# A three-layer transformer stack on one core: return of x in quarters, pool sums on DVE, resting places of the modulation stream

## Chip, cores and metric

The kernel runs on one core of a Trainium2 chip. The metric is the device time of one execution in microseconds (us). The engines are named as in the profile: PE (TensorE), PEld (its weight loads), DVE (VectorE), ACT (ScalarE), POOL (GpSimd) and SP (SyncE, which here only issues DMAs).

## What is computed

A sequence of 512 tokens of width 2048 passes three layers, all in float32. Cut to what matters (layer 1 is attention, layer 2 pooling, layer 3 stick-breaking attention and retention; A, B are head groups):

```python
def modulation(c, w, b):                       # w: 2048 x 6144
    m = silu(c) @ w + b
    return m[:D], m[D:2*D], m[2*D:]            # shift, scale, gate

# layer 1
h = rmsnorm(x, pre_g) * (1 + scale) + shift
q, kv, z = split(h @ w_in)                     # 8 + 8 heads of 128, 2 + 2 kv heads
y = concat(dense_attention(qA, kA, vA), window_attention(qB, kB, vB, sink)) * silu(z)
x = x + gate * rmsnorm(y @ w_out, post_g)

# layer 2
u, z = split(h @ w_in)                         # 2048 + 2048
for g, w in enumerate((2, 4, 8, 16)):          # 4 groups of 512 columns
    mean = (sum of u over the tokens t - w//2 .. t + w//2 - 1, clipped) / count
    mixed_g = (mean - u_g) @ pool_w[g]
y = mixed * pool_scale * silu(z)
x = x + gate * rmsnorm(y @ w_out, post_g)

# layer 3
q, k, v, z = split(h @ w_in_2)                 # 8 stick-breaking, 8 retention heads
y = concat(stick_breaking(q, k, v), group_norm(retention(q, k, v))) * silu(z)
x = x + gate * (y @ w_out_2)
```

## The kernel before, in words

Activations lie transposed in SBUF: 16 tiles of 128 features by 512 tokens. To keep float32 accuracy every product is three products of rounded parts: an operand is split into a high part (HHI, WHI, PHI) and the rest (HLO, WLO, PLO), and hi x hi, lo x hi and hi x lo are added up in a PSUM bank G. Weights come in chunks of 128x4x256 (512 KB): SP loads a chunk into RAW, ACT casts it to WHI, DVE subtracts to WLO (stage "split"; three buffers each, so the split of chunk i+2 is asked for behind chunk i and waits until PE is done with chunk i-1), PE multiplies (stage "mm", 24 matmuls of 512 columns per chunk). A unit is 4 chunks and gives two G banks.

The order of all work is written out once by `make_plan` as one list of stages; each engine walks the list and executes its part of each stage, so the list is the order in every queue. Inside it run generators: those in `background` are stepped behind every quarter of a chunk (`step(background)`), the generator `mods` once behind every chunk (`unit`, L344). `finish` and `gated` run a generator to its end.

**Modulation.** `mod_stream` (L429) has 28 jobs of 8 steps. A step is a DMA of 512 KB into MWIDE (SP, asked for two steps ahead) and two DVE instructions that add a weighted row block to MACC (`mod_acc`); behind a job PE transposes MACC and DVE reduces it (`mod_sum`). `need_mods(t)` runs the stream on at once if job t isn't summed. `at["hold"]` stops the steps; before, it is set only in the first half of layer 3. Layer 1 has the units K and V (V token-major, `gemm_tok`, 72 matmuls of 256 columns per chunk), then 8 pairs of heads, each a q unit and a z unit with the attention of the pair in the background; the last z unit also has `first_splits`, which turns Y (the layer's gated result) into HHI and HLO for the output product.

**Output product.** `project_out` begins with `gemm_two`, which has the two first output units in the chunk order TWO, so that the last four tiles of Y are needed only from the seventh chunk. At that chunk `tail` finishes the background and puts four `x_back`: POOL issues four DMAs of 1 MB that bring the residual x from DRAM back to the quarters of XR, each with a semaphore `back[q]`. They wait until the scratch area under XR is free. In layers 1 and 2 the stage `o_more` (DVE) reads XR, in layer 3 the stage `o_copy` (DVE, `Y<-G,MOD,XR`), which also frees the G bank for PE; `write_out` sends the result out in four parts.

**Pool layer.** For group g: units u (2), the pool product of group g-1 (2 units of one chunk), units z (2). While the z units run, `pool_group(g)` is in the background: pairs on DVE (`pool_first`, UP 2172 columns), then g levels of doubling on POOL (`pool_level`), then on DVE the product with 1/count and the difference to u (`pool_mean`, both in one stage), then the splits PHI (ACT) and PLO (DVE).

Of the kernel before, what the change touches and what calls it, by code (L numbers as in the profile page):

```python
# [79 lines left out]
def build(nc, ctx, T, out):  # L80
# [137 lines left out]
    g_sum, g_ux, g_pad, g_pool = on_chip("g_sum", "g_ux", "g_pad", "g_pool")  # L218
# [93 lines left out]
    def make_plan():  # L312

        todo = []
        background = []
        gates = [[], []]
        at = {"load": 0, "split": 0, "use": 0, "unit": 0, "pair": 0, "heads": False, "hold": False}
# [32 lines left out]
        def unit(work, quiet=False):  # L350
            u = at["unit"]
            at["unit"] += 1
            n = len(units[u])
            at["pair"] += n // 8 + 1
            for c in range(n):
                i = at["use"]
                at["use"] += 1
                while at["split"] <= i:
                    split_next()
                work(u, i, c, c == n - 1)  # L360
                if not at["heads"]:
                    reduce_pending()
                while at["split"] < min(i + NS, len(chunks)):
                    split_next()
                if not (quiet and c >= n - 2 or at["hold"]):
                    step([mods])
            return u
# [35 lines left out]
        def gemm_two(layer, tail):  # L403
            first = at["pair"] % 2
            gated(first)

            def work(u, i, c, last):
                uu, k0 = TWO[c]
                pair = (first + uu) % 2
                if c == 3:  # L410
                    gated(pair)
                if c == 6:
                    tail()
                for nt in range(2):
                    for jj in range(2):
                        put("mm2", "y", layer, u, i, uu, k0, nt, jj, pair)
                        step(background)

            return unit(work), first
# [9 lines left out]
        def mod_stream():  # L429
            for _ in range(4):  # L430
                yield
            put("mod_load", 0)
            put("mod_load", 1)
            yield
            for t in range(len(mod_jobs)):
                for c in range(8):
                    reduce_pending()
                    put("mod_acc", t, c)
                    if 8 * t + c + 2 < 8 * len(mod_jobs):
                        put("mod_load", 8 * t + c + 2)  # L440
                    if c < 7:
                        yield
                pending.append(t)
                yield
            reduce_pending()
# [101 lines left out]
        pair = at["pair"] % 2  # L547
        u = gemm_tok(1, 6, pair)
        for i in range(3):
            put("v_copy", 1, i, pair, u)  # L550
# [76 lines left out]
        for p in range(8):  # L627
# [7 lines left out]
            if p == 7:  # L635
                h_unit = at["unit"]
                background.append(first_splits(1))
            u, pair = gemm("h", 1)
            silu(1, 2 * p, pair, u)

        def project_out(layer, h_unit):
            def tail():
# [5 lines left out]
                for q in range(4):  # L648
                    put("x_back", layer, q)

            u, first = gemm_two(layer, tail)
            for uu in range(2):
                for nt in range(2):
                    put("o_copy", layer, 2 * uu + nt, (first + uu) % 2, nt, u, (u, "two", uu, nt))
            more = products(layer, range(4), 3)
# [58 lines left out]
        def pool_group(g):  # L714
            put("pool_first", g)
            yield
            yield
            for level in range(g):
                put("pool_level", g, level)
                for _ in range(4):  # L720
                    yield
            put("pool_mean", g)
            for _ in range(5):
                yield
# [16 lines left out]
        for g in range(4):  # L741
# [5 lines left out]
            else:  # L747
                for uu in range(2):
                    u, pair = gemm("h", 2)
                    finish(task)  # L750
# [4 lines left out]
            background.append(task)  # L755
            for uu in range(2):
# [5 lines left out]
        finish(task)  # L762
        pool_product(3)
# [187 lines left out]
    def pool_program(e):  # L951
# [17 lines left out]
        for stage, *a in plan:  # L969
# [8 lines left out]
            elif stage == "x_back":  # L978
                layer, q = a
                scratch_free(layer)  # L980
                e.wait_ge(spill, layer)
                e.o.dma_start(XR[:, 4 * q:4 * q + 4, :], XS.ap()[:, 4 * q:4 * q + 4, :]).then_inc(
# [34 lines left out]
            elif stage == "pool_level":  # L1017
                g, level = a
                cur, nxt, lo, hi, sh = level_of(g, level)
                if level:  # L1020
                    e.wait_ge(g_pool, (g, level - 1))
                else:
                    e.wait_ge(v_pool, (g, "pairs"))
                add(UP[nxt][:, :, lo:hi], UP[cur][:, :, lo - sh:hi - sh], UP[cur][:, :, lo + sh:hi + sh]).then_inc(
                    *g_pool.up((g, level)))
# [352 lines left out]
    def dve_program(e):  # L1378
# [37 lines left out]
        for stage, *a in plan:  # L1416
# [307 lines left out]
            elif stage == "pool_first":  # L1724
                g, = a
                e.wait_ge(a_ev, ("u", g, 3))
                if g:
                    e.wait_ge(v_pool, (g - 1, "lo", 3))
                tt(UP[1][:, :, 1:544], UP[0][:, :, 0:543], UP[0][:, :, 1:544], ADD).then_inc(
                    *v_pool.up((g, "pairs")))  # L1730
            elif stage == "pool_mean":
                g, = a
                cur, dst = 3 - pooled_in(g), UP[pooled_in(g)][:, :, 16:528]
                if g:
                    e.wait_ge(g_pool, (g, g - 1))
                else:
                    e.wait_ge(v_pool, (g, "pairs"))
                e.wait_ge(rcd, g)
                for j in range(4):
                    tt(dst[:, j, :], UP[cur][:, j, 16:528], RC[:, :], MUL).then_inc(*v_pool.up((g, "rc")))  # L1740
                e.wait_ge(v_pool, (g, "rc"))
# [543 lines left out]
```

## Time and profile before

| | |
|---|---|
| time, median of 3 runs | 2621.2 us (2620.88 to 2621.57) |
| time of the profiled execution | 2625.44 us |
| its span | 2623.7 us |
| busy PE, PEld | 2551.8 us (97%), 2067.8 us (79%) |
| busy DVE, ACT, POOL | 1609.3 us (61%), 942.9 us (36%), 132.8 us (5%) |
| matmuls into G with 512 columns | 3 x 2624, mean 392 to 420 ns |
| chain that ended last, by engine | PE 87%, DVE 6%, DMA 3% |
| mean granted TensorE clock | 0.982 of full speed |

The span is what lies between the first and the last instruction; the time around it is 1.7 us more. A busy share is the time in which an engine had an instruction in work. Matmuls are pipelined: one of 512 columns lasts about 0.39 us and the next starts 0.23 us after it.

### The profile page before, as it was taken

How to read it: one execution, taken by the hardware profiler on the slowest of the kernel's cores; microseconds unless marked ns; L12 is line 12 of the kernel's file. 1: busy time of each engine (PE TensorE's matmuls, PEld its weight loads, DVE VectorE, ACT ScalarE, POOL GpSimd, SP SyncE). 2: the span in 40 equal slices, each digit the busy share in tenths (PEclk: the TensorE clock that was granted, in tenths of full speed). 3: DMA queues.
4: the chain of work that ended last, by engine and by line, in shares of the span. 5: the costliest groups of instructions: out<-in, count | busy, mean ns of one | idle time of the engine just before them, and what ended most of it. 6: DMA issues, size and time to landing. Idle time of an engine off the chain costs nothing.

```text
span 2623.7 us, 31292 instructions
## 1 busy us (share of the span) xinstructions
PE 2551.8 (97%) x12627; PEld 2067.8 (79%) x12627; DVE 1609.3 (61%) x2393; ACT 942.9 (36%) x1501; POOL 132.8 (5%) x121
## 2 busy tenths in 40 slices
PE   7999999999999999999999998999999999999998
PEld 4779777777777877888777887887888878878786
DVE  4445666677777768575787667446455567546432
ACT  4222444444444333332333333445354323223221
POOL 0000000000001103001021102000000000000000
PEclk8999999999999989999999998999999999999999
DMA  9934433444446644665647563222222255422432
GB/s 350 341 120 152 124 110 112 121 129 129 129 129 226 206 146 164 206 193 164 216 157 265 177 193 132 80 89 73 79 74 89 78 172 176 141 88 93 156 109 72
DMA packets 301074, 390.67 MB, mean 149 GB/s; under 512 B 11698, under 2 KB 237618, under 8 KB 297090
## 3 DMA queue, kind: packets, MB, share of 16 engines
q1 hardware_dynamic: 294800, 354.79, 43.3%
q0 software_dynamic: 6128, 33.89, 3.4%
q8 instruction: 100, 1.64, 0.3%
q14 instruction: 44, 0.36, 0.0%
q10 hardware_dynamic: 2, 0.00, 0.0%
HBM read 371.85 MB, written 16.78 MB: 148 GB/s over the span
## 4 chain that ended last, share of the span: by engine, by line
PE 87%; DVE 6%; DMA 3%; issue 1%; ACT 1%; SPq 1%; POOL 0%; DVEq 0%; ACTq 0%; POOLq 0%
PE G L1855 73%; PE S L1855 6%; PE OB L1855 5%; PE TB L1855 2%; PE TB L1858 2%; DVE MACC L1389 1%; DMA LATE<-in_ev_mod_w 1%; DMA MRAW<-in_ev_mod_w 1%; DVE WLO L1383 1%; DVE Y L1383 1%; DMA RAW<-in_w_out 1%; SPq L935 0%; DMA MWIDE<-in_w_ada 0%; PE OB L1858 0%; DMA MORE<-in_ev_mod_w 0%
## 5 line engine op out<-in xcount | busy, mean ns | idle before, releaser
L1855 PE MATMUL G<-HHI,WHI 128*128 128x512 f32 x2624 | 1102.5, 420 | 30.5 <-issue 7.8
L1855 PE MATMUL G<-HHI,WLO 128*128 128x512 f32 x2624 | 1032.2, 393 | 0.0
L1855 PE MATMUL G<-HLO,WHI 128*128 128x512 f32 x2624 | 1029.1, 392 | 0.0
L1383 DVE TENSOR_TENSOR WLO<-RAW,WHI 128x1024 fp32r<-128x1024 f32 x376 | 463.9, 1237 | 325.8 <-ACT WHI L1064 322.8
L1064 ACT ACTIVATE WHI<-RAW 128x1024 fp32r<-128x1024 f32 x376 | 395.7, 1054 | 605.4 <-PE G L1855 545.1
L1855 PEld LDWEIGHTS G<-HHI,WHI 128*128 128x128 f32 x2624 | 497.2, 189 | 147.2 <-issue 25.6
L1855 PEld LDWEIGHTS G<-HLO,WHI 128*128 128x128 f32 x2624 | 497.7, 190 | 110.6 <-issue 14.6
L1855 PEld LDWEIGHTS G<-HHI,WLO 128*128 128x128 f32 x2624 | 495.9, 189 | 109.0
L1389 DVE SCALAR_TENSOR_TENSOR MACC<-MWIDE,SC,MACC 128x512 f32<-128x512 f32 x420 | 339.6, 809 | 25.8 <-DMA MWIDE<-in_w_ada 11.1
L1855 PE MATMUL G<-WHI,HHI 128*128 128x256 f32 x640 | 185.3, 289 | 0.0
L1855 PE MATMUL G<-WLO,HHI 128*128 128x256 f32 x640 | 181.0, 283 | 0.0
L1855 PE MATMUL G<-WHI,HLO 128*128 128x256 f32 x640 | 181.0, 283 | 0.0
L1855 PEld LDWEIGHTS G<-WHI,HHI 128*128 128x128 f32 x640 | 122.5, 191 | 7.2 <-issue 6.3
L1855 PEld LDWEIGHTS G<-WHI,HLO 128*128 128x128 f32 x640 | 122.6, 192 | 1.9 <-issue 1.0
L1855 PEld LDWEIGHTS G<-WLO,HHI 128*128 128x128 f32 x640 | 122.6, 192 | 0.0
L1061 ACT ACTIVATE SQ<-SQ 128x512 f32<-128x512 f32 x144 | 90.8, 631 | 72.7 <-DVE SQ L1389 69.7
L1855 PE MATMUL S<-KTA,QR 128*128 128x256 f32 (+2 forms) x256 | 84.0, 451 | 2.6 <-ACT PB L1206 2.6
L1855 PE MATMUL OB<-PT,VV 128*128 128x512 f32 (+2 forms) x192 | 74.7, 539 | 0.0
L1206 ACT ACTIVATE PB<-S,SM 128x512 f32<-128x512 f32 (+1 forms) x32 | 23.7, 741 | 136.1 <-DVE SM L1386 136.1
L1386 DVE TENSOR_SCALAR TM<-TB 128x512 f32<-128x512 f32 (+1 forms) x28 | 18.8, 672 | 85.7 <-ACT TY L1061 85.7
L1855 PEld LDWEIGHTS S<-KTA,QR 128*128 128x128 f32 x256 | 47.9, 191 | 29.5 <-issue 15.3
L1206 ACT ACTIVATE PB<-S,SM,COL 128x768 f32<-128x768 f32 x32 | 31.7, 992 | 109.0 <-DVE SM L1386 109.0
(268 smaller groups left out, 2335.0 us busy)
## 6 DMA issues: line engine op xcount, KB each, us to landing
RAW<-in_w_in SPq DMA_DIRECT2D x128, 512.0 KB, 3.8
MWIDE<-in_od_mod_w SPq DMA_DIRECT2D x96, 512.0 KB, 4.7
MWIDE<-in_w_ada SPq DMA_DIRECT2D x96, 512.0 KB, 4.8
RAW<-in_ev_w_in SPq DMA_DIRECT2D x80, 512.0 KB, 3.6
RAW<-in_od_w_in SPq DMA_DIRECT2D x64, 512.0 KB, 3.8
MWIDE<-in_ev_mod_w SPq DMA_DIRECT2D x32, 512.0 KB, 4.6
RAW<-in_ev_w_out SPq DMA_DIRECT2D x32, 512.0 KB, 4.3
RAW<-in_od_w_out SPq DMA_DIRECT2D x32, 512.0 KB, 4.1
```

Of the source, the lines that this page charges most:

```text
L1061: return e.o.activation(o, i, fn, bias=bias, scale=scale)
L1064: return e.o.activation(o, i, ACT.Copy, scale=scale)
L1206: e.o.activation(PB[n % 2][:, lo:768], S[:, lo:768], ACT.Exp, bias=nm, scale=1.0 if banded(h) else q_root_of(h, qt), accum_out=SM[:, i + 1 ...
L1383: return e.o.tensor_tensor(o, a, b, op)
L1386: return e.o.tensor_scalar(o, a, s1, s2, op0, op1) if op1 else e.o.tensor_scalar(o, a, s1, None, op0)
L1389: return e.o.scalar_tensor_tensor(out=o, in0=a, scalar=s, in1=b, op0=op0, op1=op1)
L1855: return e.o.matmul(o, l, r, start=start, stop=stop, skip_group_check=True)
L1858: return e.o.transpose(o, i, IDN[:, :])
```

## The change

Three parts. (1) `tail` asks only for the first quarter of x; a generator asks for the other three, each 8 background steps (two chunks) apart, and every `x_back` also waits on PE until the chunk before the current one is done. (2) `pool_level` moves from POOL to DVE, `pool_mean` is cut into `pool_mean` and `pool_diff`, and the stages of `pool_group` stand 4 background steps apart (3 in group 3). (3) `mod_stream` starts without its four empty steps; it makes a second step behind each chunk of the V unit and behind the second chunk of each u unit of groups 1 to 3; it rests from the last z unit of the heads to the fourth chunk of `gemm_two`, and during the z units of group 3.

```diff
@@ -215,7 +215,7 @@
         "v_silu")
     v_ysp, v_ux, v_tile, v_pool, v_res, v_st, v_out, v_xy = on_chip(
         "v_ysp", "v_ux", "v_tile", "v_pool", "v_res", "v_st", "v_out", "v_xy")
-    g_sum, g_ux, g_pad, g_pool = on_chip("g_sum", "g_ux", "g_pad", "g_pool")
+    g_sum, g_ux, g_pad = on_chip("g_sum", "g_ux", "g_pad")
 
     XS = nc.dram_tensor("x_spill", [P, KT, SEQ], F32)
     MUL, ADD, SUB, MAX, MIN = ALU.mult, ALU.add, ALU.subtract, ALU.max, ALU.min
@@ -314,7 +314,7 @@
         todo = []
         background = []
         gates = [[], []]
-        at = {"load": 0, "split": 0, "use": 0, "unit": 0, "pair": 0, "heads": False, "hold": False}
+        at = {"load": 0, "split": 0, "use": 0, "unit": 0, "pair": 0, "heads": False, "hold": False, "extra": ()}
         scored = []
         summed = set()
         pending = []
@@ -364,6 +364,8 @@
                     split_next()
                 if not (quiet and c >= n - 2 or at["hold"]):
                     step([mods])
+                    if c in at["extra"]:
+                        step([mods])
             return u
 
         def gemm(kind, layer, quiet=False):
@@ -409,6 +411,8 @@
                 pair = (first + uu) % 2
                 if c == 3:
                     gated(pair)
+                if c == 4:
+                    at["hold"] = False
                 if c == 6:
                     tail()
                 for nt in range(2):
@@ -427,8 +431,6 @@
             return unit(work)
 
         def mod_stream():
-            for _ in range(4):
-                yield
             put("mod_load", 0)
             put("mod_load", 1)
             yield
@@ -545,7 +547,9 @@
         task = chain([norm_rope(("k", 2), False), norm_rope(("k", 3), False)])
         background.append(task)
         pair = at["pair"] % 2
+        at["extra"] = (0, 1, 2, 3)
         u = gemm_tok(1, 6, pair)
+        at["extra"] = ()
         for i in range(3):
             put("v_copy", 1, i, pair, u)
         finish(task)
@@ -635,6 +639,7 @@
             if p == 7:
                 h_unit = at["unit"]
                 background.append(first_splits(1))
+                at["hold"] = True
             u, pair = gemm("h", 1)
             silu(1, 2 * p, pair, u)
 
@@ -645,13 +650,19 @@
                 if layer == 2:
                     for k in range(12, KT):
                         put("y_split", layer, k, h_unit)
-                for q in range(4):
-                    put("x_back", layer, q)
+                put("x_back", layer, 0, at["use"] - 2)
+
+            def rest_back():
+                for q in range(1, 4):
+                    for _ in range(8):
+                        yield
+                    put("x_back", layer, q, at["use"] - 2)
 
             u, first = gemm_two(layer, tail)
             for uu in range(2):
                 for nt in range(2):
                     put("o_copy", layer, 2 * uu + nt, (first + uu) % 2, nt, u, (u, "two", uu, nt))
+            background.append(rest_back())
             more = products(layer, range(4), 3)
             for uu in range(2, 8):
                 if layer == 3:
@@ -712,16 +723,20 @@
         put("pads")
 
         def pool_group(g):
+            apart = 3 if g == 3 else 4
             put("pool_first", g)
+            for _ in range(apart):
+                yield
+            for level in range(g):
+                put("pool_level", g, level)
+                for _ in range(apart):
+                    yield
+            put("pool_mean", g)
+            for _ in range(apart):
+                yield
+            put("pool_diff", g)
             yield
             yield
-            for level in range(g):
-                put("pool_level", g, level)
-                for _ in range(4):
-                    yield
-            put("pool_mean", g)
-            for _ in range(5):
-                yield
             for j in range(4):
                 put("pool_split", g, j)
                 if j % 2:
@@ -746,13 +761,16 @@
                         put("u_copy", 0, 2 * uu + nt, (first + uu) % 2, nt, (u, "two", uu, nt))
             else:
                 for uu in range(2):
+                    at["extra"] = (1,)
                     u, pair = gemm("h", 2)
+                    at["extra"] = ()
                     finish(task)
                     for nt in range(2):
                         put("u_copy", g, 2 * uu + nt, pair, nt, (u, nt))
                 pool_product(g - 1)
             task = pool_group(g)
             background.append(task)
+            at["hold"] = g == 3
             for uu in range(2):
                 if g == 3 and uu == 1:
                     h_unit = at["unit"]
@@ -760,6 +778,7 @@
                 u, pair = gemm("h", 2)
                 silu(2, 4 * g + 2 * uu, pair, u)
         finish(task)
+        at["hold"] = False
         pool_product(3)
 
         need_mods(4 + 11)
@@ -976,9 +995,10 @@
                 e.o.dma_start(XS.ap()[:, 4 * q:4 * q + 4, :], XR[:, 4 * q:4 * q + 4, :]).then_inc(
                     *spill.up((1, q), *([1] if q == 3 else []), by=16))
             elif stage == "x_back":
-                layer, q = a
+                layer, q, i = a
                 scratch_free(layer)
                 e.wait_ge(spill, layer)
+                e.wait_ge(p_gemm, i)
                 e.o.dma_start(XR[:, 4 * q:4 * q + 4, :], XS.ap()[:, 4 * q:4 * q + 4, :]).then_inc(
                     *back[q].up(layer, by=16))
             elif stage == "o_copy":
@@ -1014,15 +1034,6 @@
                 if g:
                     e.wait_ge(v_pool, (g - 1, "rc"))
                 e.o.dma_start(RC[:, :], T["t_rcnt"][g]).then_inc(*rcd.up(g, by=16))
-            elif stage == "pool_level":
-                g, level = a
-                cur, nxt, lo, hi, sh = level_of(g, level)
-                if level:
-                    e.wait_ge(g_pool, (g, level - 1))
-                else:
-                    e.wait_ge(v_pool, (g, "pairs"))
-                add(UP[nxt][:, :, lo:hi], UP[cur][:, :, lo - sh:hi - sh], UP[cur][:, :, lo + sh:hi + sh]).then_inc(
-                    *g_pool.up((g, level)))
             elif stage == "tables3":
                 e.wait_ge(*x_done(2, 0))
                 e.o.dma_start(CS[:, :], T["t_rope_b"][0]).then_inc(*rope.up("cs3", by=16))
@@ -1728,16 +1739,22 @@
                     e.wait_ge(v_pool, (g - 1, "lo", 3))
                 tt(UP[1][:, :, 1:544], UP[0][:, :, 0:543], UP[0][:, :, 1:544], ADD).then_inc(
                     *v_pool.up((g, "pairs")))
+            elif stage == "pool_level":
+                g, level = a
+                cur, nxt, lo, hi, sh = level_of(g, level)
+                e.wait_ge(v_pool, (g, "level", level - 1) if level else (g, "pairs"))
+                tt(UP[nxt][:, :, lo:hi], UP[cur][:, :, lo - sh:hi - sh], UP[cur][:, :, lo + sh:hi + sh], ADD).then_inc(
+                    *v_pool.up((g, "level", level)))
             elif stage == "pool_mean":
                 g, = a
                 cur, dst = 3 - pooled_in(g), UP[pooled_in(g)][:, :, 16:528]
-                if g:
-                    e.wait_ge(g_pool, (g, g - 1))
-                else:
-                    e.wait_ge(v_pool, (g, "pairs"))
+                e.wait_ge(v_pool, (g, "level", g - 1) if g else (g, "pairs"))
                 e.wait_ge(rcd, g)
                 for j in range(4):
                     tt(dst[:, j, :], UP[cur][:, j, 16:528], RC[:, :], MUL).then_inc(*v_pool.up((g, "rc")))
+            elif stage == "pool_diff":
+                g, = a
+                dst = UP[pooled_in(g)][:, :, 16:528]
                 e.wait_ge(v_pool, (g, "rc"))
                 tt(dst, dst, UP[0][:, :, 16:528], SUB).then_inc(*v_pool.up((g, "mean")))
             elif stage == "pool_split":
```

## Rows read from the trace of the kernel before

**Rows 1.** Waits of TensorE: releaser, us in total, times, longest us

```profile
PE G L1855 <- DVE Y L1389: 8.1, 3, 6.1
```

**Rows 2.** Timeline of TensorE: start us, us, instruction, [idle before <-releaser]

```profile
775.42 0.59 PE L1855 MATMUL S<-KTA,QR 128*128 128x384 f32 x1 [2.56 <-ACT PB L1206]
793.48 0.50 PE L1855 MATMUL G<-HHI,WHI 128*128 128x512 f32 x1 [3.98 <-DVE HLO L1383]
1248.25 0.50 PE L1855 MATMUL G<-HHI,WHI 128*128 128x512 f32 x1 [1.16 <-DVE WLO L1383]
1255.57 0.50 PE L1855 MATMUL G<-HHI,WHI 128*128 128x512 f32 x1 [1.59 <-DVE WLO L1383]
1351.61 0.50 PE L1855 MATMUL G<-HHI,WHI 128*128 128x512 f32 x1 [2.17 <-DVE WLO L1383]
1368.94 0.33 PE L1858 MATMUL TB<-IDN,MACC 128*128 128x128 f32 x1 [0.67 <-DVE MACC L1389]
1391.07 0.50 PE L1855 MATMUL G<-PHI,WHI 128*128 128x512 f32 x1 [1.83 <-DVE Y L1389]
2472.64 0.76 PE L1855 MATMUL G<-HHI,WHI 128*128 128x512 f32 x1 [6.10 <-DVE Y L1389]
```

**Rows 3.** Windows: busy us per engine, then PEclk, DMA share, GB/s

```profile
794.00:799.00 5.00, 5.00 (x17) 3.89 (x17) 2.48 (x5) 0.28 (x1) 0.00 (x0) 0.66 0.54 168
1391.00:1396.00 5.00, 4.93 (x15) 3.90 (x16) 5.00 (x9) 2.49 (x5) 0.02 (x1) 0.66 0.24 88
2472.60:2477.60 5.00, 4.96 (x14) 4.01 (x15) 1.87 (x3) 0.60 (x1) 0.28 (x1) 0.51 0.35 105
2458.00:2462.00 4.00, 4.00 (x19) 3.34 (x18) 1.40 (x2) 0.00 (x0) 0.00 (x0) 1.00 1.02 421
1232.00:1276.00 44.00, 41.25 (x181) 33.53 (x180) 40.29 (x40) 14.95 (x21) 9.36 (x3) 1.00 0.57 175
```

**Rows 4.** Timeline of DVE at the end of the heads

```profile
770.55 1.53 DVE L1389 SCALAR_TENSOR_TENSOR MACC<-MWIDE,SC,MACC 128x512 f32<-128x512 f32 x2
779.33 1.53 DVE L1389 SCALAR_TENSOR_TENSOR MACC<-MWIDE,SC,MACC 128x512 f32<-128x512 f32 x2
792.74 0.69 DVE L1383 TENSOR_TENSOR HLO<-Y,HHI 128x512 fp32r<-128x512 f32 x1
```

**Rows 5.** Window of one chunk of the token-major V unit

```profile
206.20:214.80 8.60, 8.60 (x74) 8.60 (x73) 3.25 (x4) 1.06 (x1) 0.00 (x0) 1.00 0.77 247
```

**Rows 6.** Timelines of POOL and DVE, pool groups 2 and 3

```profile
1237.62 8.88 POOL L953 TENSOR_TENSOR UP<-UP 128x2164 f32<-128x2164 f32 x2 [93.93 <-DVE UP L1383]
1238.58 8.47 DVE L1389 SCALAR_TENSOR_TENSOR MACC<-MWIDE,SC,MACC 128x512 f32<-128x512 f32 x2
1337.41 8.48 DVE L1389 SCALAR_TENSOR_TENSOR MACC<-MWIDE,SC,MACC 128x512 f32<-128x512 f32 x2
1345.81 5.75 DVE L1383 TENSOR_TENSOR WLO<-RAW,WHI 128x1024 fp32r<-128x1024 f32 x1
```

**Rows 7.** Groups of DVE by line: busy us, mean ns, idle before

```profile
L1383 DVE TENSOR_TENSOR WLO<-RAW,WHI 128x1024 fp32r<-128x1024 f32 x376 | 463.9, 1237 | 325.8 <-ACT WHI L1064 322.8
L1383 DVE TENSOR_TENSOR UP<-UP,RC 128x512 f32<-128x512 f32 x16 | 10.0, 686 | 0.0
L1383 DVE TENSOR_TENSOR UP<-UP 128x2172 f32<-128x2172 f32 x4 | 9.7, 2414 | 3.7 <-ACT UP L1064 3.7
L1383 DVE TENSOR_TENSOR UP<-UP,UP 128x2048 f32<-128x2048 f32 x4 | 9.2, 2292 | 0.1
```

**Rows 8.** Chain that ended last, eight chunks of 24 matmuls: start, us

```profile
1278.08 43.56 PE G L1855 x192
```

**Rows 9.** Timelines of POOL and ACT in the last output product

```profile
2454.11 2.10 POOL L982 DMA_DIRECT2D XR<-x_spill  x4 [33.28 <-issue]
2469.52 1.06 ACT L1064 ACTIVATE WHI<-RAW 128x1024 fp32r<-128x1024 f32 x1 [13.01 <-DMA RAW<-in_w_out]
```

**Rows 10.** View of tile XR, 2440 to 2480, four returns of x

```profile
DMA to landing us min/median/max: 5.2/9.2/13.5
```

## The prediction

> **What bounds the kernel now.** I read the profile in this order: the table of engine busy time, the waits of TensorE, the timeline of TensorE around each of them, then the timelines of DVE, ACT and POOL just before. TensorE (PE) is busy 97% of the span and almost every piece of the chain that ends last is a matmul into a G bank, so a step is worth something only if it removes time in which PE stands still, or a stretch at the lower clock behind it. DVE is busy 61%: its mean says nothing, its place in each PE wait does.
>
> In the stages that the diff touches, PE has eight waits over 0.5 us [rows 1, 2]; the others lie in the intro, at the two layer boundaries and in the retention heads. Two lie at the end of the heads (2.56 and 3.98 us), two in pool group 2 (1.16, 1.59), three in and behind pool group 3 (2.17, 0.67, 1.83), and one in the last output product (6.10, the largest of the three waits of [rows 1]). Together 20.1 us. Behind three of them the granted clock is lower for a while: in 5 us it is 0.66 behind 793.5, 0.66 behind 1391, 0.51 behind 2472.6 [rows 3]. A share of 0.66 is part of the 5 us at 1.2 and the rest at 2.4 GHz. That costs 5 x 0.34 = 1.7, 1.7, and 5 x 0.49 = 2.45 us, 5.85 in all. The most the change could give is thus 25.9 us.
>
> **Modulation rests at the end of the heads.** One step of the modulation is two DVE instructions on MACC, 1.53 us together and 1.45 from its start to the start of what follows [rows 4]. Before: one step behind each chunk. After: none behind the four chunks of the last z unit and the first four of the output product; they are made up by starting four chunks earlier and by a second step in each of four chunks of the token-major V unit. Counting the generator through: before, 106 chunk steps up to the end of the layer-1 output less 5 that only load make 101 accumulations; after, 106 + 4 - 8 less 1, again 101. Twelve jobs need 96, so need_mods pulls nothing forward, and in the heads the count is exactly 8 higher, the same phase of a job. In the V unit PE waits for nothing in the trace and DVE is busy 3.25 of the 8.6 us that a chunk takes [rows 5], so the steps added there (two per chunk, 2.9 us) are hidden; if that cover were short, a late WLO would cost PE at most one step, 1.5 us.
>
> At 772.9 PE waits for scores whose exp waits for DVE. With the step at 770.55 gone DVE can run the split at once, but the silu piece behind it still waits for ACT: I trace it to about 772.0 instead of 772.69, so 0.7 is gained of 1.45. At 789.5 PE waits for the last of the y splits before its third chunk, DVE 792.74 [rows 4]. From 776 to 793 DVE works nearly without pause, so the removed step at 779.33 moves it by its whole 1.45, on top of the 0.7. Sum 2.2 us. The waits that stay (about 4.3 us) are softmax round trips between DVE and ACT. The lower clock behind them may stay too, I count half: 0.85. Bounds: 0 and 6.5 + 1.7.
>
> **Running sums on DVE.** POOL takes 4.4 us for one level, and meanwhile DVE's modulation step, 1.53 us elsewhere, lasts 8.47 and 8.48 us, and one split 5.75 instead of 1.24 [rows 6, 7]. So the level costs DVE nearly POOL's whole time though it runs on POOL: 8.47 - 1.53 = 6.9 us in group 2, and 6.95 + 4.5 = 11.5 us in group 3. A level on DVE isn't in the trace; the same form with 8 columns more is, 2.41 us [rows 7]. Six levels at 2.4 (1, 2, 3 in groups 1 to 3) put 4.8 us on DVE in group 2 and 7.2 in group 3 in place of 6.9 and 11.5. Bounds of a level: 2.3 (the subtraction of 2048 columns, [rows 7]) and 4.4, POOL's.
>
> The Trainium skill, SBUF — State Buffer, section "SBUF: two separate sides", says that DVE and GpSimd share one port pair by an exclusive lock, whoever starts first holding it for its whole instruction. By that rule the cost in group 2 is POOL's full 8.9 us less what was already running, against 6.9 from the row; the trace agrees. By the same rule a level on DVE would hold POOL in turn, and POOL has nothing there but one small table load.
>
> The larger part is order. In group 2 the split of the fourth chunk is queued behind POOL's two levels, and the next behind mean and difference at once: hence 1.16 and 1.59. After, the stages stand 4 steps, one chunk, apart. Eight chunks of 24 matmuls take 43.56 us, one 5.45 [rows 8]; DVE's work in it is split 1.24 + step 1.45 + level 2.41, or mean 4 x 0.63 (0.69 each, overlapping a little) in its place: 5.2 at most. A split is two chunks ahead and can start when the chunk before is done: with 1.06 for ACT's WHI and its own 1.24 about 8 us of room. The first chunk of the second z unit holds difference, four splits of the pool, one silu and a split and step: 8.5 us, which that room covers with about 0.5 us to spare. Over the stretch DVE is already 40.3 of 44 us busy [rows 3], 6.9 of it blocked, so I keep 0.5 us of new wait. Group 2 gives 2.75.
>
> In group 3 the spacing is 3 and the modulation rests for the eight chunks, 8 x 1.45 = 11.6 us of DVE less on top of 11.5 - 7.2 = 4.3. The tightest point is now the first chunk, with pairs, one level and its split due 10.9 us in; they end about 10.5 us in (today DVE starts the pairs 4.6 us into group 2, behind the same kind of job sum that group 3 gets now: + 2.33 + 2.33 + 1.2). DVE then stays ahead, the silu before the last pool product starts some 4 us earlier, and the waits 2.17, 0.67 and 1.83 go: 4.67 us, with the 1.7 us of lower clock. The two extra steps per group 1 to 3 stand in u chunks where DVE has only a split and then two steps, 1.24 + 2.9 of 5.45 us; their loads were issued a chunk before. The count is 163 instead of 165 behind group 3, and 193 instead of 195 where 192 are needed: nothing is forced. Pools together: 2.75 + 4.67 + 1.7 - 0.5 = 8.6. Bounds: 0 and 9.1.
>
> **Return of x in quarters.** Four DMAs of 1 MB already exist; all are issued at 2454.1 to 2455.7. The weight load issued beside them lands 14 us later, so WHI waits 13.01 us for it [rows 9], and DVE's split and then its first Y follow in order: PE stands from 2466.54. With the engines of the DMA at 421 GB/s [rows 3], 4 MB + 0.5 MB need 11 us; 1 MB + 0.5 MB need 3.7. The first quarter landed in 5.2 even in the crowd [rows 10]. After: the first quarter waits until the sixth chunk is done (about 2455.4, 1.3 later) and lands by 2462; the load lands by 2461; WHI may start when its buffer is free, chunk 7 done, 2461.1; WLO to 2463.5, Y to 2464.2; PE needs it at 2466.5. The wait of 6.10 goes with 2.3 us to spare, and the clock stays up: 2.45. Sum 8.55. Bounds 0 and 8.55 (the first quarter as late as 13.5 us gives nothing). What is behind the new wait in POOL's queue: the copies of x_out and, in layers 1 and 2, the adds of squares. Quarter 1 is issued when the second chunk of the next unit is done and needed (o_more 4, or o_copy 4 in layer 3) 11 us later at the earliest; at 5 to 9 us per quarter that holds by 2. In layers 1 and 2 no PE wait follows the burst now, so nothing is gained there.
>
> **Sum.** 2.2 + 0.85 + 8.6 + 8.55 = 20.2 us. The profiled execution took 2625.44 us (span 2623.7), so 2605.2 for it; it stands 4.2 above the median 2621.2, which gives 2601.
>
> **Rivals.**
> (1) The end of layer 3 is held by DVE's order or by the first quarter itself, not by the load: PE still waits 3 to 6 us and the clock falls. For it: Y also needs back[0]. Against: 5.2 us of landing. Gives 2.5 instead of 8.55: 2607. Chance 0.10.
> (2) The pools stay bound by DVE: the busy share of 0.92 and the 0.5 us margins speak for it, the removed blocking against it. Pools give 1: 2609. Chance 0.10.
> (3) Slower. In the first two chunks of the second z unit of groups 1 to 3, ACT and DVE pass silu and pool splits to and fro, with a level's worth of work more queued on DVE; if each of these six chunks is 4.5 us late, PE stands 27 us and the clock falls three times, 5 us: 32 in place of the pools' 9.1, against 2.2 + 0.85 + 8.55 = 11.6 gained elsewhere, so 11.3 slower, 2632.5. It decides from 3.5 us per chunk (21 + 5 - 9.1 - 11.6 = 5.3). Against it: group 1 has no wait today although its POOL level blocks DVE. Chance 0.05.
> (4) The change does nothing measurable: waits move to the next dependency everywhere. Chance 0.05: 2619.
>
> **How the numbers follow.** Forecast 0.70. What the measurement tells from no change is about 0.2%, 5.2 us. Faster: forecast, (1), (2): 0.90; same 0.05; slower 0.05. Range: all waits and clocks gone, 2595.3, would be the bottom; the top takes in (1) and (2) with some of both, 2612. Range 2595 to 2612.
>
> **What would show it.** Right: no PE row with a wait from 2440 to 2500 and a granted clock of 1.00 there; WHI's wait for w_out gone; MACC pairs at 1.5 us and DVE UP rows of 2.4 us one chunk apart; no WLO wait from 1230 to 1395; the wait of 3.98 down to about 2.6. Wrong: a PE wait on WLO in a second z unit, a Y of the last product waiting for XR, o_more waiting for XR in layers 1 or 2, or waits of PE for WLO in the first 100 us behind the intro.

## The result, and the profile after

The changed kernel takes 2612.57 us (median of 7 runs, 2606.37 to 2614.91), the kernel before beside it 2621.05 (7 runs). The ratio is 0.9965, 95% interval 0.9956 to 0.9975: 9 us faster, where 20.2 were forecast, and 0.57 us above the range.

The profiled execution took 2612.22 us (span 2610.1), close to its median. That of before lay 4.2 us above its own, so the two profiles differ by 13.2 us (13.6 in span). I aligned the two traces by their matmuls into G (10,032 in each) and read how far the one is ahead at each place. Less than 0 is a gain, in us (rounded; the lines add up to 13.4):

```
stretch                          profiles   forecast   PE waits that went or came
up to the last heads                -1.1        0
end of the heads                    -4.9      -3.05    2.56 went; 3.98 became 2.92
first layer boundary                +1.4        0      none came
pool groups 2 and 3                -10.8      -8.6     1.16, 1.59, 2.17, 0.67, 1.83 went
layer-2 output product              +6.2        0      3.99 CAME
second boundary, score heads        +0.1        0
retention heads                     +4.3        0      0.88, 0.36, 1.07, 0.88 CAME
layer-3 output product              -8.6      -8.55    6.10 went
```

So what was meant to go went, and two new groups of waits came. Waits of TensorE after (releaser, us in total, times, longest us). The row of [rows 1] for Y is gone. A row for HLO has two waits in it, of which the longer is new, and rows for MACC and WLO stand for the retention heads:

```profile
PE G L1872 <- DVE HLO L1394: 6.9, 2, 4.0
PE TB L1875 <- DVE MACC L1400: 1.8, 2, 0.9
PE G L1872 <- DVE WLO L1394: 1.4, 2, 1.1
```

Timeline of TensorE after, the rows that answer to [rows 2] and the new ones:

```profile
787.63 0.79 PE L1872 MATMUL G<-HHI,WHI 128*128 128x512 f32 x1 [2.92 <-DVE HLO L1394]
1417.31 0.77 PE L1872 MATMUL G<-HHI,WHI 128*128 128x512 f32 x1 [3.99 <-DVE HLO L1394]
2128.99 0.66 PE L1875 MATMUL TB<-IDN,MACC 128*128 128x128 f32 x4 [0.88 <-DVE MACC L1400]
2191.64 0.50 PE L1872 MATMUL G<-HHI,WHI 128*128 128x512 f32 x1 [0.36 <-DVE WLO L1394]
2198.45 0.50 PE L1872 MATMUL G<-HHI,WHI 128*128 128x512 f32 x1 [1.07 <-DVE WLO L1394]
2232.51 0.65 PE L1875 MATMUL TB<-IDN,MACC 128*128 128x128 f32 x4 [0.88 <-DVE MACC L1400]
```

Windows after (busy us per engine, PEclk, DMA share, GB/s). The places of [rows 3] in pool group 3, the last output product and group 2: 1.00 in all three, and DVE 37.0 us busy over group 2 (40.3 before). The third row is the new wait: half of 5 us idle, the rest near 1.2 GHz. Behind the wait that stays at the heads (787.63) the granted clock is 0.72 over 5 us, 0.66 before.

```profile
1384.00:1389.00 5.00, 5.00 (x24) 4.14 (x23) 3.63 (x6) 1.06 (x1) 0.00 (x0) 1.00 0.78 263
2460.00:2465.00 5.00, 5.00 (x28) 4.13 (x27) 1.31 (x2) 0.60 (x1) 0.55 (x1) 1.00 0.30 95
1415.00:1420.00 5.00, 2.69 (x6) 2.15 (x7) 4.96 (x8) 0.00 (x0) 0.00 (x0) 0.55 0.89 321
1226.00:1270.00 44.00, 44.00 (x197) 36.40 (x196) 37.02 (x41) 16.98 (x23) 0.54 (x1) 1.00 0.56 168
```

What DVE does ahead of the new wait (timelines of DVE and POOL after):

```profile
1413.35 0.69 DVE L1521 TENSOR_REDUCE MOD<-TB 128x4 f32<-128x512 f32 x1 [7.49 <-PE TB L1875]
1413.45 0.53 POOL L1002 DMA_DIRECT2D XR<-x_spill  x1 [168.65 <-PE G L1872]
1414.16 1.22 DVE L1394 TENSOR_TENSOR WLO<-RAW,WHI 128x1024 fp32r<-128x1024 f32 x1
1415.30 0.48 DVE L1397 TENSOR_SCALAR MACC<-MWIDE,SC 128x512 f32<-128x512 f32 x1
1415.81 0.75 DVE L1400 SCALAR_TENSOR_TENSOR MACC<-MWIDE,SC,MACC 128x512 f32<-128x512 f32 x1
1416.48 2.49 DVE L1394 TENSOR_TENSOR HLO<-Y,HHI 128x512 fp32r<-128x512 f32 x4
```

Every eighth modulation step ends a job. PE then transposes MACC (L1875) and DVE sums the result (`mod_sum`, L1521). DVE works two chunks ahead of PE, so it stands for 7.49 us until PE has come to these transposes. Behind the sum in DVE's queue are a split, the next job's first step and only then the four splits HLO 12 to 15. PE wants these directly behind its transposes: it waits from 1413.32 to 1417.31. Before, the sum lay two chunks earlier in the order (timeline of DVE before):

```profile
1417.93 0.69 DVE L1510 TENSOR_REDUCE MOD<-TB 128x4 f32<-128x512 f32 x1 [2.28 <-PE TB L1858]
1428.13 2.49 DVE L1383 TENSOR_TENSOR HLO<-Y,HHI 128x512 fp32r<-128x512 f32 x4
```

In the retention heads it is another neighbour, read off the two traces alone. The job's last step (MACC, 2127.41) is queued behind a chain of DVE work that begins at 2122.03, and PE, which is to transpose this MACC, waits 0.88 us for it:

```profile
2122.03 0.69 DVE L1397 TENSOR_SCALAR TM<-TB 128x512 f32<-128x512 f32 x1 [0.97 <-ACT TY L1072]
2127.41 1.53 DVE L1400 SCALAR_TENSOR_TENSOR MACC<-MWIDE,SC,MACC 128x512 f32<-128x512 f32 x2
```

Counted in the order of work (c=0 is the first chunk), the layer-2 output product has these DVE stages behind its third to sixth chunk, and the last line just ahead of its seventh, which reads HLO 12 to 15:

```
        before (165 steps ahead)      after (163 steps ahead)
c=2     last step of job 20           step
c=3     SUM, step                     step
c=4     step                          last step of job 20
c=5     step                          SUM, step
c=6     splits 12-15, x_back          splits 12-15, x_back
```

### The profile page after: what moved, and what is told of

The parts are those of the page before. It is cut to its first block, busy times and chain, and to the rows that moved or that the text cites. A ratio compares the mean times of both kernels' runs of the same rounds, so it can differ in the third digit from the quotient of the medians.

```text
span 2610.1 us, 31294 instructions
## 1 busy us (share of the span) xinstructions
PE 2548.2 (98%) x12627; PEld 2067.6 (79%) x12627; DVE 1601.3 (61%) x2399; ACT 943.6 (36%) x1501; POOL 104.6 (4%) x115
## 4 chain that ended last, share of the span: by engine, by line
PE 91%; DVE 4%; DMA 2%; ACT 1%; SPq 1%; issue 1%; POOL 0%; DVEq 0%; POOLq 0%; ACTq 0%
PE G L1872 76%; PE S L1872 6%; PE OB L1872 5%; PE TB L1872 2%; PE TB L1875 2%; DMA MORE<-in_ev_mod_w 1%; DMA LATE<-in_ev_mod_w 1%; SPq L954 1%; DVE WLO L1394 0%; DVE Y L1394 0%; PE OB L1875 0%; DMA MRAW<-in_ev_mod_w 0%; DVE TT L1394 0%; DMA RAW<-in_ev_w_in 0%; DVE HLO L1400 0%
## 5 line engine op out<-in xcount | busy, mean ns | idle before, releaser
L1394 DVE TENSOR_TENSOR WLO<-RAW,WHI 128x1024 fp32r<-128x1024 f32 x376 | 458.4, 1221 | 308.9 <-ACT WHI L1075 305.7
L1400 DVE SCALAR_TENSOR_TENSOR MACC<-MWIDE,SC,MACC 128x512 f32<-128x512 f32 x420 | 322.0, 767 | 38.0 <-DMA MWIDE<-in_w_ada 14.7
L1521 DVE TENSOR_REDUCE MOD<-TB 128x4 f32<-128x512 f32 x28 | 19.3, 689 | 84.0 <-PE TB L1875 84.0
```

What stands on the lines that cost most here:

```text
L1394: return e.o.tensor_tensor(o, a, b, op)
L1400: return e.o.scalar_tensor_tensor(out=o, in0=a, scalar=s, in1=b, op0=op0, op1=op1)
L1521: e.o.tensor_reduce(m, TB[:, :].rearrange("p (n k) -> p n k", n=4), AX_X, ADD).then_inc(*v_msum.up(t))
```

## The experiments

Three theories of what took the gain. **Phase**: eight steps are rested in group 3 and six put back, so every later sum of a job comes two chunks later, at worse places. **Quarters**: the first return of x is now issued at that same chunk (1413.45) and waits for it, so the quarters or the wait hold it. **Execution**: the waits or their clock belong to this execution. Each ratio below is to the kernel before, run on the same chip, and in it the difference of one profiled execution plays no part.

**The kernel before again.**

> The kernel before itself, unchanged, as a second execution in the profile. The pair of profiled executions differs by 13.2 us (2625.44 and 2612.22), the medians by 8.5. If the profiled execution of before was an unusual one (granted clock at a layer boundary or in the intro), this one stands within 1 us of the median of its timed runs, near 2621, and a comparison of its matmul times with the first trace names the place of some 4 us. If instead the profile always costs before 4 us, it gives 2625 again and the 4 us belong to something that the change removes only under the profiler. Timed against before: ratio 1.000, within 0.001.

Measured: 2622.16 us, 2616.92 to 2625.12 over 10 runs; ratio 1.000 (0.9991 to 1.0009). The profiled one took 2619.39, so 2625.44 was an execution from the top of what this kernel shows, and no cost of profiling. The two traces of one program part by 6.1 us; 4.6 of these come between 1340 and 1745, at the end of group 3 and at the second layer boundary, where some waits differ and the clock stays lower for longer or shorter, and about 1 each way at the heads and the first boundary. A ledger of two single traces is no better than this wherever a stretch at the lower clock is part of it. Most waits repeat better: of [rows 2], 2.57, 3.97, 1.15, 1.58, 1.96, 1.59 and 6.05 here, and 0.67 not at all. Others do not. The waits for HLO at the two layer boundaries are 2.58 and 2.61 in the first trace and 1.55 and 1.55 in the second, and the 3.98 at 793.48 is 2.00, 3.03, 3.07, 3.12 and 3.26 in the five kernels below that leave the heads as they were.

**Two more steps.**

```diff
-                    at["extra"] = (1,)
+                    at["extra"] = (1, 3) if g == 3 else (1,)
```

> The changed kernel with two more modulation steps, one each in the fourth chunk of the two u units of pool group 3, so that 165 accumulations (not 163) stand ahead of the layer-2 output product, as in the kernel before. Theory (the phase of the modulation job): the job's sum is again queued two chunks earlier, after the third chunk of the product, the PE wait of 3.99 us for HLO at its seventh chunk and the half clock behind it go (6.6 us), and in the retention heads the four waits of 0.88, 0.36, 1.07 and 0.88 us go too (4.25 us with what lies around them): about 2612.6 - 10.9 = 2601.7 us, at most 2604. Rival (the quartered return of x, whose first DMA waits for a chunk of the product at that very place): the wait for HLO stays, only the retention part goes, 2608. Rival (chance of that execution, the clock): no difference, 2612.

Measured: 2596.91 us, ratio 0.9906 (0.9892 to 0.9919). More work at the same places makes the changed kernel 15 us faster. DVE has waited the same 7.49 us for its sum, but now two chunks ahead of the splits (timeline of DVE, this kernel):

```profile
1399.85 0.69 DVE L1521 TENSOR_REDUCE MOD<-TB 128x4 f32<-128x512 f32 x1 [7.49 <-PE TB L1875]
1404.11 1.53 DVE L1400 SCALAR_TENSOR_TENSOR MACC<-MWIDE,SC,MACC 128x512 f32<-128x512 f32 x2
1408.31 1.54 DVE L1400 SCALAR_TENSOR_TENSOR MACC<-MWIDE,SC,MACC 128x512 f32<-128x512 f32 x2 [0.59 <-DMA MWIDE<-in_w_ada]
1409.76 2.49 DVE L1394 TENSOR_TENSOR HLO<-Y,HHI 128x512 fp32r<-128x512 f32 x4
1411.32 0.54 POOL L1002 DMA_DIRECT2D XR<-x_spill  x1 [169.12 <-PE G L1872]
```

PE has no wait at the seventh chunk and none of the four of the retention heads; of HLO only the one at the end of the heads is left (2.9, once):

```profile
PE G L1872 <- DVE HLO L1394: 2.9, 1, 2.9
```

The quarters are as in the changed kernel (POOL issues the first at 1411.32, right behind its chunk), so they are not what took the gain. In the retention heads the job's sum now stands at 2103.78, ahead of the chain (TM at 2109.48). The gain is 5 us more than expected. The profiles of the changed kernel and of this one are 17.3 us apart: 6.4 in the output product and 4.3 in the retention heads, 10.7 where 10.9 were expected, and 6.6 over both boundaries, the heads and the intro, which is of the size that one program shows against itself. Of the 6.6, 3.6 lie at the second layer boundary.

**Two steps less in the kernel before**, and nothing else:

```diff
-                if not (quiet and c >= n - 2 or at["hold"]):
+                if not (quiet and c >= n - 2 or at["hold"] or at.get("skip") == c):
...
+                    at["skip"] = 3 if g == 3 else None
                     u, pair = gemm("h", 2)
+                    at["skip"] = None
```

> The kernel before with nothing of the change, only two modulation steps left out of the u units of pool group 3 (its fourth chunk, twice), so that 163 accumulations instead of 165 stand ahead of the layer-2 output product; they are made up by the stream's end. DVE has less to do there, no other instruction moves. Theory (phase): PE waits some 4 us for HLO at the seventh chunk of the layer-2 product, with a lower clock behind it, and four waits of together 3.2 us appear in the retention heads: +6.6 + 4.25 = 10.9 us, 2622 + 10.9 = 2632.5. Rival (the new waits come with the quartered return of x or with the levels on DVE): 2621 to 2623. A rival between: only the retention waits come (2626).

Measured: 2636.14 us, ratio 1.0051 (1.0039 to 1.0063). Less work for DVE makes the kernel before 13 us slower (10.9 expected). The two rows of TensorE below are new against it, and the row of DVE is a job's sum that stood two chunks earlier there:

```profile
1436.92 0.76 PE L1857 MATMUL G<-HHI,WHI 128*128 128x512 f32 x1 [3.99 <-DVE HLO L1385]
2146.89 0.66 PE L1860 MATMUL TB<-IDN,MACC 128*128 128x128 f32 x4 [0.88 <-DVE MACC L1391]
1333.18 0.69 DVE L1512 TENSOR_REDUCE MOD<-TB 128x4 f32<-128x512 f32 x1 [5.24 <-PE TB L1860]
```

The same 3.99 and 0.88 as after, with the old return of x and POOL's levels. The third row is a place that the changed kernel does not suffer from: with this sum close ahead of them, group 3's pairs start at 1337.50, for 1332.99 in the second trace of before (PE itself is 0.8 later), and the PE wait behind them grows from 1.96 to 5.62 us. A shift of two steps has three places in which it costs.

**The splits ahead of the sum.** One step moves inside the output product; the counts ahead of and behind it stay 163 and 193 (`skip` is read as in the run above):

```diff
+            at["skip"], at["extra"] = (4, (7,)) if layer == 2 else (None, ())
             u, first = gemm_two(layer, tail)
+            at["skip"], at["extra"] = None, ()
```

> The changed kernel with one modulation step moved inside the layer-2 output product, from the fifth chunk to the eighth: the splits 12 to 15 then stand ahead of the job's sum in DVE's queue, though the count is still 163 ahead and 193 behind. Theory (it is the sum, which waits for PE's transposes, ahead of the splits that PE needs next): the wait of 3.99 us for HLO in the seventh chunk and its lower clock go (6.4 us), the retention waits stay (4.25 us): 2612.6 - 6.4 = 2606, range 2604 to 2608. If the seventh chunk is late for another reason (the chunk's own WLO, the first quarter of x): 2612.

Measured: 2604.99 us, ratio 0.9930 (0.9918 to 0.9943), inside the range that was expected, though its six runs lie in two clumps, 2600.1 to 2602.2 and 2607.8 to 2608.7, and the profiled one is the highest. In the trace the wait of 3.99 is gone, 6.6 us are gained from the start of the product on, and the retention waits of 0.88, 0.36, 1.03 and 0.88 stay, with 4.3 us over that stretch against "two more steps". So the two places are separate, and in the first it is the order of sum and splits.

**One more step.** As "two more steps", in the first unit only, 164 ahead.

> The changed kernel with one more modulation step in a u unit of group 3: 164 accumulations ahead of the layer-2 output product, the job's sum between its fourth and fifth chunk, one chunk ahead of the last splits. Theory: the sum then waits for PE one chunk earlier and the splits 12 to 15 stand one chunk free of it: the wait of 3.99 us goes; in the retention heads the sum comes one chunk step off the 163 place, I take half of 4.25 us: 2597 + 2 = 2599. If any shift against 165 costs: 2604 to 2608, between 163 and 165. If 164 is as bad as 163: 2612.

Measured: 2602.53 us (2599 expected), ratio 0.9927 (0.9915 to 0.9940). The wait is there, but shorter; over the retention heads 0.8 us are lost instead of 4.3:

```profile
1415.29 0.47 PE L1872 MATMUL G<-HHI,WHI 128*128 128x512 f32 x1 [1.12 <-DVE HLO L1394]
```

I had expected one chunk to be room enough, and it was not, by this 1.12. The wait falls step by step, 163, 164, 165: 3.99, 1.12, none.

**Without the rest beside group 3**, and so without its six second steps:

```diff
-                    at["extra"] = (1,)
                     u, pair = gemm("h", 2)
-                    at["extra"] = ()
...
-            at["hold"] = g == 3
```

> The changed kernel without its rest beside pool group 3 and without the six second steps that make up for it; levels on DVE, spacing, the rest at the heads and the quartered return stay. The kernel with the pool part alone showed no PE wait in groups 2 and 3, so the rest there is not needed, and without it the count is 165: 2596.9 +- 2 us, the same as with two more steps added. If the rest does carry something in group 3 when the stream has another phase: waits on WLO there, 2600 to 2605.

Measured: 2598.54 us, ratio 0.9908 (0.9895 to 0.9921), the same as with two more steps. No PE wait on WLO from 1200 to 1400. The rest beside the last group brought nothing, and its count of six for eight cost what was lost. This and "two more steps" are the fastest versions, 24 us below before.

**The parts alone, on the kernel before.** First the return of x in quarters:

> The kernel before with the return of x in quarters and nothing else of the change. By the ledger of the two traces: the wait of 6.10 us in the layer-3 output product goes with the lower clock behind it, 8.6 us; no new wait in the layer-2 product, because the phase of the modulation is that of before: 2621 - 8.6 = 2612.4 us, 2611 to 2614. If the quartering itself caused the new wait of 3.99 us in the layer-2 product: 2619. If DVE's order alone holds the layer-3 end: 2618 to 2621.

Measured: 2611.23 us, ratio 0.9962 (0.9948 to 0.9975), 10 us. The window of the last output product has no gap in PE and full clock, and the layer-2 product has no wait:

```profile
2440.00:2500.00 60.00, 59.98 (x271) 48.90 (x270) 26.55 (x30) 17.84 (x22) 4.32 (x8) 1.00 0.53 170
```

Then the rest at the heads:

> The kernel before with the rest at the end of the heads alone: stream started four chunks earlier, four second steps in the token-major V unit, eight steps left out at the end of the heads. By the traces so far: the wait of 2.57 us goes and that of 3.0 to 4.0 us stays at 2.9, and part of the lower clock behind it goes: -5.0 to -6.4 us, 2616.5. The prediction's own term was 2.2 + 0.85 = 3.05: 2619.

Measured: 2619.07 us, ratio 0.9985 (0.9977 to 0.9994), 3.9 us (1.6 to 6). The trace gains 6.2 at the heads against the second trace of before and gives 2.5 back at the first layer boundary. Of the two numbers I had, the prediction's own (3.05) was nearer, though the interval holds 5.0 as well.

Then the pools, without rest:

> The kernel before with the running sums on DVE and the spacing of the pool's stages, without rests or extra steps of the modulation and with the old return of x. Theory: the waits of 1.16 and 1.59 us in group 2 go (2.75). In group 3 the seven modulation steps stay on DVE, 11.6 us more than with the rest, against 4.3 us less blocking; the waits of 2.17, 0.67 and 1.83 us there stay in part, I take half with the clock stretch, so 2.75 + 2 = 4.8 us: 2616, range 2613 to 2619. If the levels on DVE and the order are all that matters and the rest is not needed: -9 to -10.8 us, 2611. If without the rest DVE falls behind in group 3: waits of over 5 us on WLO there, 2621 or more.

Measured: 2613.96 us, ratio 0.9970 (0.9959 to 0.9981), 7.9 us. My "half" was too low: both groups are free of waits without the rest, as in the changed kernel.

The product of the three ratios is 0.9917; with the count back at 165 the whole change gives 0.9906 and 0.9908. Within their intervals the parts add up, and what was missing was the phase.

**Levels or order.** The pool part with one half of it each:

> The pool part alone, but with the levels left on POOL: only the spacing (stages four chunk steps apart, three in group 3, difference apart from the mean) is new against the kernel before. Theory of the prediction (the larger part is order): the waits of 1.15 and 1.58 us in group 2 and some of 1.96 and 1.59 us in group 3 go, -4 to -6 us, 2617, while DVE is still held by POOL's levels. Rival (what holds DVE is the length of POOL's levels): the held DVE instructions of 8.5 us stay, waits on WLO of 1 us and more stay in both groups, 2620 to 2623, or longer, since the later mean pushes the pool's splits towards the second z unit: 2625.

> The pool part alone with the levels on DVE, but in the order of the kernel before (two steps behind pairs, four behind a level, mean and difference together, five behind them). Theory (levels of 2.4 us on DVE in place of 8.5 us in which DVE is held are enough): all waits in groups 2 and 3 go as with the spacing, -7.9 us, 2614.5. Rival of the prediction (order): the wait behind mean and difference (1.58 us) and part of group 3 stay, -3 us, 2619.

The edit of the second in `pool_group`, against the kernel before (cut; `pool_level` goes to DVE and `pool_diff` is a stage of its own, as in the change):

```diff
             put("pool_mean", g)
+            put("pool_diff", g)
             for _ in range(5):
                 yield
```

Measured: spacing alone 2620.44 us, ratio 0.9987 (0.9978 to 0.9996), 3.4 us; levels on DVE alone 2614.95, ratio 0.9973 (0.9961 to 0.9984), 7.1 us, of the 7.9 of both. The two intervals just overlap, and 7.1 and 7.9 cannot be told apart. With spacing alone POOL's levels still lengthen DVE's work as in [rows 6] (timelines of POOL and DVE):

```profile
1334.19 14.04 POOL L957 TENSOR_TENSOR UP<-UP 128x2164 f32<-128x2164 f32 x3 [78.77 <-DVE UP L1387]
1335.15 8.47 DVE L1393 SCALAR_TENSOR_TENSOR MACC<-MWIDE,SC,MACC 128x512 f32<-128x512 f32 x2
1343.55 5.77 DVE L1387 TENSOR_TENSOR WLO<-RAW,WHI 128x1024 fp32r<-128x1024 f32 x1
1349.37 0.50 PE L1862 MATMUL G<-HHI,WHI 128*128 128x512 f32 x1 [1.96 <-DVE WLO L1387]
```

In the old order with DVE's levels, two waits are left of five. They are what the spacing adds in the trace, 1.9 us:

```profile
1253.15 0.50 PE L1853 MATMUL G<-HHI,WHI 128*128 128x512 f32 x1 [0.85 <-DVE WLO L1375]
1383.97 0.50 PE L1853 MATMUL G<-PHI,WHI 128*128 128x512 f32 x1 [1.01 <-DVE Y L1381]
```

## Why the prediction was wrong, by its steps

- **"The count is 163 instead of 165 behind group 3, and 193 instead of 195 where 192 are needed: nothing is forced."** This is the step that failed. The counts are right and nothing is forced. But I used them only to ask whether `need_mods` pulls steps forward, and not where 163 modulo 8 puts the next sum. For the heads I had noted that the phase stays the same, and did not ask the same here. Price: 6.2 us in the layer-2 product and 4.3 in the retention heads by the trace; 15 us (0.9906 against 0.9965) by the ratios, so some 5 more. Of these, 3.6 stand at the second layer boundary in both kernels that have the count at 165 and the rest of the change, against the trace of the changed one; the kernel before with two steps less shows no loss there (0.3 against the second trace of before), so it is not shown that they belong to the phase. None of the four rivals had it: all looked at the places that the diff touches.
- **"In layers 1 and 2 no PE wait follows the burst now, so nothing is gained there."** No gain from the quarters, right. I took it for nothing happening there and did not look at what else stands in DVE's queue at that chunk.
- **Return of x.** 8.55 forecast, 8.6 in the trace, 10 (6.6 to 13.6) timed alone. POOL issues the first quarter at 2450.95, the four quarters of this product land in 5.0 to 7.2 us (median 5.2), WHI waits only for its buffer (4.73, released by PE, at 2456.27), PE not at all.
- **Running sums.** 8.6 forecast, 10.8 in the trace, 7.9 timed alone: right in sum, wrong in its split. "The larger part is order" fell: the levels' place alone gives 7.1 us, the order alone 3.4, both together 7.9. A level on DVE takes 2.40 us as estimated (row below, whole kernel, ten of them with the four pairs), and MACC is back at 1.53 us. The 0.5 us kept for a new wait was not needed, and neither was the rest of the modulation, on which the text laid 11.6 us of DVE's room: here DVE had room, and more of it gained nothing.

```profile
L1394 DVE TENSOR_TENSOR UP<-UP 128x2172 f32<-128x2172 f32 (+3 forms) x10 | 24.0, 2402 | 3.7 <-ACT UP L1075 3.7
```

- **End of the heads.** 3.05 forecast, 3.9 timed alone. The split between the two waits was wrong: the first (2.56) went wholly, where I gave it 0.7. It stands at 2.56 to 2.58 in all seven traces without the rest at the heads and in none with it. The second went from 3.98 to 2.92, but with the heads left as they were it is anything from 2.00 to 3.98, so a gain there is not shown.
- **What would show it.** Of the signs named for "right", all but one are in the trace: full clock and no wait from 2440 to 2500, no WHI wait for w_out, UP rows of 2.4 us (one chunk apart in group 2), no WLO wait from 1230 to 1395. The wait of 3.98 is 2.92 and not "about 2.6". None of those named for "wrong" is there. A list of signs for the touched places could not have caught this.

The Trainium skill, SBUF — State Buffer, section "SBUF: two separate sides", says that DVE and GpSimd hold their port pair in turn, the one that starts first for its whole instruction. The runs agree as far as GpSimd holds DVE: with the levels on POOL the two MACC instructions of a step last 8.47 us however the stages are spaced, with the levels on DVE 1.53. That DVE holds GpSimd in its turn no run here shows.

Left open: the 5 us between traces and ratios for the phase, and why the first layer boundary gives back 1.4 to 2.6 us in most traces whose heads end earlier, but not in that of "two more steps". Two traces of one program differ by 1 us there, which is not enough to tell.

## What to carry to other kernels

A stream of small steps that is laid between other work has a period as well as a length. Here every eighth step brings an instruction that makes DVE stand for up to 7.5 us, so before steps are taken out or added, follow the stream's phase to the end of the kernel and look at each stage that needs its data soon behind such an instruction. When work is rested, put back as many steps as were left out, or, which no run here tried, as many as make a whole period. And before an engine is relieved, ask whether the places in question wait for its load or for one long hold: here taking POOL's hold away gave most of it.

## What was not expected of the hardware

A stretch with a wait and the lower clock behind it differs between executions of one program by more than its waits do. Between 1340 and 1745 us the two traces of the kernel before part by 4.6 us, and of that the waits make 2.2 (1.96 for 2.17, 1.59 for 1.83, 0.67 gone, and at the second layer boundary 1.55 for 2.61). The rest is in how long PE runs at the lower clock. These are the 6.6 us behind the last of the waits at the second boundary, in the first trace and in the second:

```profile
1597.40:1604.00 6.60, 6.56 (x16) 5.16 (x17) 6.47 (x9) 2.33 (x3) 2.53 (x2) 0.52 0.40 161
1595.00:1601.60 6.60, 6.60 (x29) 5.45 (x30) 6.46 (x9) 2.33 (x3) 2.55 (x2) 1.00 0.40 161
```

From 1760 to 2440 us, where the granted clock is 1.00, the same two traces agree to 0.03 us.
